# Earlier loads and shorter stage boundaries around the latent attention of a hybrid decoder, with six extra multiplications by TensorE in a wait

## The reference, cut to what matters

```
h = rmsnorm(x)
u = h @ w_in                       # columns: SSD | RWKV-7 | latent attention (MLA)
o_ssd, o_rwkv, o_mla = three mixers on u
gates = sigmoid(h @ w_gate + b_gate)
x = x + (gates0*(o_ssd@w_o_ssd) + gates1*(o_rwkv@w_o_rwkv) + gates2*(o_mla@w_o_mla)) @ w_out
x = x + ConvFFN(rmsnorm(x))
```

```
k = rmsnorm([c @ w_kb, rope_key]);  sc = q . k * scale           # per head, all 16 pages and the new tokens
pr = softmax(sc);  acc = pr @ c;  o_mla = acc @ w_vb
```

## Time and profile before

| what | value |
|---|---|
| median of 3 runs | 2997.09 us (2993.64 to 3005.37) |
| the profiled execution's own time | 2993.64 us |
| its span | 2991.5 us |
| TensorE busy | 2687.4 us, 90% |
| VectorE busy | 1881.6 us, 63% |
| ScalarE busy | 1351.0 us, 45% |
| GpSimd busy | 843.0 us, 28% |
| mean granted TensorE clock | 0.946 of full speed |

### The profile page before, as it was taken

The page is one execution under the profiler, slowest core; times in us unless marked ns, Lnnn a source line. Parts: engine busy times, 40 slices in busy tenths (PEclk is TensorE's granted clock), DMA queues, the critical chain, the costliest instruction groups (busy, mean ns, idle before and its releaser), DMA issues. The chain is left out here.

```text
span 2991.5 us, 62010 instructions
## 1 busy us (share of the span) xinstructions
PE 2687.4 (90%) x24068; PEld 2459.3 (82%) x24068; DVE 1881.6 (63%) x3141; ACT 1351.0 (45%) x2290; POOL 843.0 (28%) x696
## 2 busy tenths in 40 slices
PE   7986879999989889899988878799999798898998
PEld 6876449999988589899877863599999795898998
DVE  4854456777766655489358454477777575554993
ACT  4733354545444244354366334355555352434542
POOL 0030007999930400000000300099999104000000
PEclk9999879999998999999989989799999898999999
DMA  5324329877545376455453243497867244764644
GB/s 134 106 63 127 112 50 163 144 123 122 83 77 159 93 199 169 113 156 144 115 128 87 75 131 103 88 152 126 139 95 116 55 144 119 189 164 105 164 137 124
DMA packets 838310, 365.86 MB, mean 122 GB/s; under 512 B 406125, under 2 KB 825494, under 8 KB 837448
## 3 DMA queue, kind: packets, MB, share of 16 engines
q1 hardware_dynamic: 835794, 360.77, 52.7%
q10 hardware_dynamic: 2232, 1.26, 0.2%
HBM read 342.63 MB, written 61.23 MB: 135 GB/s over the span
## 5 line engine op out<-in xcount | busy, mean ns | idle before, releaser
L1196 PE MATMUL key_banks<-w_kb_head,latent_T_head 128*128 128x352 f32 x1536 | 520.5, 339 | 32.1 <-DVE latent_T_rest L1343 27.6
L1196 PE MATMUL key_banks<-w_kb_rest,latent_T_head 128*128 128x352 f32 x1536 | 496.9, 323 | 0.0
L1196 PE MATMUL key_banks<-w_kb_head,latent_T_rest 128*128 128x352 f32 x1536 | 496.2, 323 | 0.0
L293 DVE TENSOR_TENSOR w_rests<-w_ring,w_heads 128x2048 fp32r<-128x2048 f32 (+1 forms) x152 | 326.4, 2150 | 166.7 <-ACT w_heads L287 166.4
L1196 PEld LDWEIGHTS key_banks<-w_kb_head,latent_T_head 128*128 128x128 f32 x1536 | 291.4, 190 | 46.1 <-issue 29.7
L1357 DVE TENSOR_REDUCE w_kb<-key_sq 128x8 f32<-128x1024 f32 x256 | 311.0, 1215 | 12.3 <-ACT key_sq L1269 7.7
L978 POOL TENSOR_TENSOR rwkv_state_tmp<-rwkv_state,vec 128x1024 f32<-128x1024 f32 x64 | 154.5, 2414 | 509.0 <-DMA rwkv_state<-in_state_rwkv_dram 504.1
L287 ACT CAST w_heads<-w_ring 128x2048 fp32r<-128x2048 f32 (+1 forms) x152 | 272.3, 1794 | 54.6 <-ACT conv_last_rows L1899 19.7
L1196 PEld LDWEIGHTS key_banks<-w_kb_rest,latent_T_head 128*128 128x128 f32 x1536 | 291.8, 190 | 0.0
L1196 PEld LDWEIGHTS key_banks<-w_kb_head,latent_T_rest 128*128 128x128 f32 x1536 | 290.4, 189 | 0.0
L1256 ACT CAST latent_T_head<-turn_bank 128x256 fp32r<-128x256 f32 x256 | 95.5, 373 | 412.2 <-PE key_banks L1200 384.4
(11 more groups left out here) (587 smaller groups left out, 6998.7 us busy)
## 6 DMA issues: line engine op xcount, KB each, us to landing
w_ring<-in_ffn_w_up_dram SPq DMA_DIRECT2D x88, 512.0 KB, 5.0
page_latents<-in_cache_kv_latent_dram SPq DMA_DIRECT2D x256, 128.0 KB, 2.4
latent_blocks<-page_latents SPq DMA_DIRECT2D x256, 128.0 KB, 3.7
latents<-page_latents SPq DMA_DIRECT2D x64, 512.0 KB, 8.8
w_ring<-in_w_in_dram SPq DMA_DIRECT2D x52, 512.0 KB, 3.7
w_ring<-in_w_gate_dram SPq DMA_DIRECT2D x48, 512.0 KB, 3.9
w_ring<-in_w_in_dram SPq DMA_DIRECT2D x20, 1024.0 KB, 6.4
w_ring<-in_ffn_w_down_dram SPq DMA_DIRECT2D x32, 384.0 KB, 3.2
```

What stands on the lines that cost most here:

```text
L293: ops.tensor_tensor(rests[:, slot, 0:tiles * P], ring[:, slot, 0:tiles * P], heads[:, slot, 0:tiles * P].bitcast(F32), ALU.subtract).then_ ...
L1196: last = nc.tensor.matmul(kbank[:, 3 * x + n, 0:KB], c[:, x, r * P:(r + 1) * P], w[:, r, cols], start=r == 0 and m == 0, stop=r == 1 and m ...
```

## The change

The diff has eight parts.

1. `rwkv_tiles`: the prompt's state goes to a buffer of its own, and SP does not wait for its store; the wait stands at the end of `mla_project`. SP loads the first quarter of the first MLA weights in `rwkv_tiles`, behind the page copies.
2. `mla_project` does not wait for its four stores; ScalarE waits for them in `mla_qkv`, ahead of its first write to their source.
3. `mla_prompt` copies eight pages in place of ten and loads the sample's RWKV states; the other two pages are copied in `cache_attention`.
4. `mla_absorb` makes the head and rest of `w_kb` and of the first two sequences' queries, and SP loads there the first two blocks, half of the first rope blocks and the sample's rows. The sixteen small instructions on the new scores become two.
5. `cache_attention` begins with the pages; four small constants are made behind the third transpose.
6. `acc @ w_vb` and its copy move to the start of `ssd_project`, into bank 6.
7. `merge`: the weights of its first unit come in four transfers. The first half of the unit (g = 0) is rounded and split in two pieces, TensorE waits for these alone, and for the second half behind it.
8. In the last sequence's tail TensorE makes six products of the identity with 512 columns of constants into a bank of the keys, which nobody reads, before it waits for the maxima.

```diff
-GATHER = {..., "prompt": range(79, 89), "cache": range(89, NB * PAGES)}
+GATHER = {..., "prompt": range(79, 87), "cache": range(87, NB * PAGES)}
@@ rwkv_tiles, sync
                 copied = gather_pages(sp, k, GATHER["tiles"], gathered)
+                sp.dma_start(k.first_w[:, :, :], k.ldram("w_in")[0:2 * P, OFF_MLA:OFF_MLA + 256]...).then_inc(k.first_in, 16)
                 sp.wait_ge(kept["st"], 2)
-                sp.dma_start(..., state_rows).then_inc(st_out, 16)
-                sp.wait_ge(st_out, 16)
+                sp.dma_start(..., state_rows[:, :, :]).then_inc(k.state_stored, 16)
@@ mla_project, sync
-                for q in range(4):
+                for q in range(1, 4):
...
-                sp.wait_ge(stored, 64)
+                sp.wait_ge(k.state_stored, 16)
@@ mla_qkv, scalar
+                act.wait_ge(k.latents_stored, 64)
                 turned_out(0)
@@ mla_prompt, sync
+                for b in range(NB):
+                    sp.dma_start(k.state[b:P:NB, :, :]..., k.ldram("state_rwkv")[b:b + 1]...).then_inc(k.rows_back, 16)
                 copied = gather_pages(sp, k, GATHER["prompt"], gathered)
@@ mla_absorb, sync
+                load_blocks(sp, k, 0)
+                load_rope_blocks(sp, k, 0, 0)
+                sp.dma_start(k.vec[:, :, :, :]..., k.vec_rows...).then_inc(k.rows_back, 16)
+                load_blocks(sp, k, 1)
@@ mla_absorb, scalar
+                nc.scalar.copy(k.wh[:, :, 32:32 + KW], k.w_kb[:, :, :]).then_inc(w_heads, 1)
                 act.wait_ge(new_made, 1)
...
+                act.wait_ge(qa_kept, 2)
+                for b, cols in enumerate(FIRST_QUERIES):
+                    nc.scalar.copy(k.wh[:, :, cols], k.qa[:, :, b, :]).then_inc(k.q_headed, 1)
@@ mla_absorb, vector
+                dve.wait_ge(w_heads, 1)
+                nc.vector.tensor_tensor(k.wl[:, :, 32:32 + KW], k.w_kb[:, :, :], k.wh[...].bitcast(F32), ALU.subtract)
                 dve.wait_ge(made, 1)
...
-                for b in range(NB): ... tensor_tensor(out, banks[...b...], bc(ss, NS), ALU.mult)
-                for b in range(NB): ... tensor_tensor(out, out, mask[...b...], ALU.add)
+                c(nc.vector.tensor_tensor(out, banks[0:NSAM, 7, 0:256]..., bc(ss[:, :], NS)..., ALU.mult))
+                c(nc.vector.tensor_tensor(out, out, mask..., ALU.add))
@@ cache_attention, tensor, finish
                     if at == TURN_TOP:
+                        if is_last(b):
+                            pe.wait_ge(taken, NB * PAGES - 1)
+                            for _ in range(6):
+                                nc.tensor.matmul(kbank[:, 0, :], k.col("ident"), k.const[:, 0:BANK], start=True, stop=True, skip_group_check=True)
                         pe.wait_ge(topped, b + 1)
...
                 seqs(pe, body, finish)
-                pe.wait_ge(divided, NB)
-                for h in range(HEADS): for r in range(2): matmul(mbank..., k.w_vb..., acc...)
@@ ssd_project, tensor and vector
+                for h in range(HEADS): for r in range(2): matmul(banks[:, 6, ...], k.w_vb..., k.qa...)
+                last.then_inc(vmade, 1)
                 for u in range(NU):
...
                 nc.vector.tensor_tensor(y, y, bc(stat2[:, :], 64), ALU.mult).then_inc(normed, 1)
+                dve.wait_ge(vmade, 1)
+                nc.vector.tensor_copy(k.o_mla[:, :, SEQ:T], banks[:, 6, 0:HEADS * NSAM]...).then_inc(v_kept, 1)
                 rest_unit(nc.vector, dve, ring, heads, rests, rounded, split, 0, 1)
@@ merge, tensor, scalar and vector
+                            if u == 0 and g == 0 and t % 4 == 0:
+                                pe.wait_ge(piece_split, t // 4 + 1)
...
-                heads_of(0)
+                for q in range(2):
+                    act.wait_ge(piece_in[q], 16)
+                    nc.scalar.copy(piece(heads, q), piece(ring, q)).then_inc(piece_rounded, 1)
+                act.wait_ge(loaded[0], 32)
+                nc.scalar.copy(heads[:, 0, 2 * HALF:4 * HALF], ring[:, 0, 2 * HALF:4 * HALF]).then_inc(rounded, 1)
...
-                rests_of(0)
+                for q in range(2):
+                    dve.wait_ge(piece_rounded, q + 1)
+                    nc.vector.tensor_tensor(piece(rests, q), piece(ring, q), piece(heads, q).bitcast(F32), ALU.subtract).then_inc(piece_split, 1)
+                dve.wait_ge(rounded, 1)
+                nc.vector.tensor_tensor(rests[:, 0, 2 * HALF:4 * HALF], ...).then_inc(split, 1)
```

More of the change, by code:

```diff
@@ L1022, in cache_attention @@
     GROUPS = len(VALUES)
-    BLK = 3
     AHEAD = 3
@@ L1229, in finish @@
                                          start=True, stop=True, skip_group_check=True).then_inc(folded, 1)
-                pe.wait_ge(w_split, 1)
-                pe.wait_ge(ready, 4)
                 seqs(pe, body, finish)
-                pe.wait_ge(divided, NB)
-                for h in range(HEADS):
-                    for r in range(2):
-                        last = nc.tensor.matmul(mbank[:, h * 32:(h + 1) * 32], k.w_vb[:, r, h * P:(h + 1) * P],
-                                                acc[:, r, :, h * NS:(h + 1) * NS], start=r == 0, stop=r == 1, skip_group_check=True)
-                last.then_inc(vmade, 1)
             @block.scalar
             def _(act):
-                nc.scalar.copy(wh[:, :, 32:32 + KW], k.w_kb[:, :, :]).then_inc(w_heads, 1)
                 def query(b, slot):
                     nc.scalar.copy(wh[:, :, query_cols(slot)], k.qa[:, :, ds(b, 1), :].rearrange("p r o c -> p r (o c)")).then_inc(q_headed, 1)
-                query(0, 0)
-                query(1, 1)
-                act.wait_ge(w_split, 1)
                 def head(b, j):
@@ L1464, in _ @@
             def _(pe):
+                for h in range(HEADS):
+                    for r in range(2):
+                        last = nc.tensor.matmul(banks[:, 6, h * NSAM:(h + 1) * NSAM], k.w_vb[:, r, h * P:(h + 1) * P],
+                                                k.qa[:, r, :, h * NS:(h + 1) * NS], start=r == 0, stop=r == 1, skip_group_check=True)
+                last.then_inc(vmade, 1)
                 for u in range(NU):
@@ L1625, in merge, with piece @@
         squared, summed, inverse, y_ready = (st.sem(n) for n in ("squared", "squares_summed", "inverse_root", "ssd_normed"))
+        HALF = DT * P // 2
+        piece_in = [st.sem(f"first_piece_loaded{q}") for q in range(2)]
+        piece_rounded, piece_split = st.sem("first_pieces_rounded"), st.sem("first_pieces_split")
+        def piece(buf, q):
+            return buf[:, 0, q * HALF:(q + 1) * HALF]
         def gate_tile(u):
```

220 lines of the change are left out of this document (118 added, 102 removed).

## The result

The changed kernel takes 2953.38 us, the median of four runs (2951.6 to 2956.12). The kernel before, on the same chip, takes 2997.36 (four runs, 2993.64 to 3005.37). The ratio is 0.9851, 95% interval 0.9829 to 0.9872: 44 us faster, 38 to 51 by the interval. Predicted were 2946 in a range of 2932 to 2966, and faster with 0.94. The profiled execution took 2951.6 (span 2949.8, mean granted clock 0.957).

What follows compares the result with a forecast made beforehand. TensorE, busy for 90% of the span, was taken as the bound, so only idle time at boundaries could be gained. Terms of 24.0 and 24.1 us a layer, together 48.1, from 2993.64 gave 2945.5, predicted as 2946, range 2932 to 2966.

Steps and rivals of the forecast that it cites:

- A: Start of the MLA stage: without waiting for the state store and with first weights loaded, 3.0 us gained a layer.
- B: End of `mla_project`: the next stage starts earlier without the wait for four stores, 1.1 us a layer (0.8 to 1.2).
- C: `mla_prompt`: SP's eight loads for two page copies cost 0, or up to 2 us if they hold it up.
- D: `mla_absorb` to the pages' start: moved heads, rests and loads let pages start earlier, 9.2 us in layer 1, 8.6 in layer 2.
- D': Second block in the page loop: TensorE's stall goes as block and states are there, 1.9 and 2.6 us by layer.
- E: `acc @ w_vb` at the start of `ssd_project`: values run in the weights' shadow, first SSD product 4.8 us earlier a layer.
- F: First unit of `merge`: first half starts at once, second half earlier, 4.0 us gained a layer (3.1 to 4.6).
- G: Six products in the last sequence's tail: 0 gained, weighted sums still at half clock; ends 3.2 gain and 3.8 loss.
- rival 2: Stage boundaries: transfers issued earlier land no earlier, and `mla_prompt` ends 2 late; 11.7 us less gain, 2957; chance 0.16.
- rival 1: Last sequence's tail: the six products keep the clock up for weighted sums and values, 3.2 us a layer, 2939; chance 0.13.
- Rival 3: Page loop: its rhythm breaks as VectorE's work becomes longer; at 0.25 us a page the kernel takes 3010; chance 0.03.
- Rival 4: Pages' start and values: something the timeline does not show holds the boundary, 21 us gain left, 2973; chance 0.05.

Runs made afterwards that it cites:

- second profile: The kernel before and the changed kernel, each unchanged, profiled once more: one run of 3008.3 us before, median 2954.31 us of five for the changed kernel.
- version with ten products: Changed kernel with eight identity products in place of six before the maxima and two more behind their spread: 2946.32 us, ratio 0.9824 to the kernel before.
- version with fill: Changed kernel with ten tail products, plus four 512-column products between the value products at the start of `ssd_project`: 2960.64 us, ratio 0.9864 to the kernel before.

## Why the prediction was right

In us for each layer:

| term | predicted | measured | from |
|---|---|---|---|
| A state store, first MLA weights | 3.0 | 2.7 to 3.3 | all waits for MLA weights, 20.5 to 15.0 (layer 1: 9.74 to 6.12, less 0.75 more ahead of a later piece); 3.3 with the waits back |
| B four stores | 1.1 | 0.9 | 4.46 to 3.60 |
| C `mla_prompt` | 0 | 0, or a loss of 2.4 | wait 1.10 to 3.50 in layer 2 of the first profile |
| D pages' start | 9.2, 8.6 | 6.9 to 9.3, mean 8.3 | `mla_absorb` to first key product: 26.95, 26.38 (second profile 26.48, 27.14) to 17.83, 19.47 (18.53, 17.84) |
| D' second block | 1.9, 2.6 | 0.9 to 3.7, mean 2.8 | stall gone; first to last key product 429.30, 431.81 (431.82, 431.77) to 428.36, 428.79 (428.08, 428.31) |
| E values | 4.8 | 5.1 | values moved back |
| F `merge` | 4.0 | 3.4 to 3.7 | whole unit; sums' start to second half 14.83 to 11.12 |
| G six products | 0 | loss of 0.7 to 1.2 in ten layers of 14, none or a gain of up to 1.2 in four | without them |

For two layers the middle values give 43 to 46, against the 48 predicted and the 44 of the medians. The spread of the single terms is mostly the clock's, so that they meet the 44 so closely is in part luck.

*What bounds.* The reading that only TensorE's idle time at boundaries could be given back held: its busy time did not fall. But the page loop did not quite keep its rhythm: it loses 1.1 to 1.6 a layer, a cost that no term of the sum has. It hides in D', where more came back than the stall: in three of the four layers of before the clock also fell once behind the stall, and in none of the changed kernel.

*The boundaries.* In the mean of the layers A, B, D and D' came out within 0.6 of the step's working. The chain from the new scores to the first key product was read rightly. Single layers differ more: D gives 6.9 where `mla_absorb` ran at the lower clock behind SP's late end. Two of the reasons are thinner than I put them: the queue at the second block was relieved twice over, and the loads alone held the start almost as long as both together, the heads for two thirds of it.

*The values.* The size is right, the working was partly luck. I took 5.23 for the values, from an execution in which a part ran at full clock; in all later profiles they run at half clock for most or all of their time. The first SSD product then stands right behind them, as predicted, but in layer 1 it comes 25.1 behind the last key product and not the 23.2 worked out, 1.8 later. That the old place would have cost as much more makes up for it.

*The six products.* The step named the right reason (a second idle stretch behind them) and put the clock's fall ahead of the weighted sums, where it was. What it missed is what the clock does next. Without them the clock has already fallen and recovers in part before the values; with them it falls later, and in ten layers of 14 all of the folds and values are slow. The Trainium skill's "TensorE: Matmul & The Clock Gate", section "What's actually happening", makes the throttled state the default that activity releases. The version with ten products bears that out as far as the weighted sums (1.00), and the values, with TensorE busy for 6.00 of 6 at 0.50, do not.

*`mla_prompt`.* Here I took 0 with up to 2 as the other end, and said I would be wrong on the mechanism if SP ended it. It did in one layer of the first profile. Why not always: behind its first instruction of the stage TensorE is done after 29.9 to 37.2 us, by the clock, and SP after 31.3 to 32.8; in the kernel before SP was done after 29.6 to 29.8, so eight loads for two page copies made its work 2 to 3 us longer. Only behind the fastest attention (29.9, in two of the 20 layers with this stage) is SP last by more than 0.2. The cost is 2.4 and a slower `mla_absorb`. The fast attention itself made the stage 4.8 shorter in that layer of the first profile; that is no effect of a term. Of rival 2 this part was right; `merge` (3.1) and MLA (2.3) fell short of what was measured, and the stall at the second block did not stay.

*Rivals.* Of rival 1 only the worth of a kept clock was right. Rival 3 was right that the rhythm of the pages can change, and wrong by far on the size: about 0.01 us a page (1 us in 80 pages) and not 0.25. TensorE is the engine that is slower in it, with no idle time, and not VectorE. The sign that I named for it, pages of more than 3.1 us, was badly chosen: 80 pages in 268.2 us are 3.35 a page in the kernel before, since the softmax and weighted sums stand between the pages; after it is 3.37. Rival 4 fell with every boundary starting earlier.

## What to carry to other kernels

At a stage boundary look at who enters it last, SP included, and count what starts only behind it: loads, roundings and small products can be moved across one at a time, but where two chains stand side by side most of the gain comes only when both are moved. In this kernel filling idle time to keep the clock up paid only where it reached up to the work that should run fast; half a fill moved the fall onto useful work in most layers. When a change of a few us a layer is measured, read it from the stage that it touches and in more than one profile, since untouched stages move by up to 6 us from one execution to the next. And compare the long loops too, however untouched they look: 1 us in 268 repeated in every profile here, and no wait shows it.

## What the runs showed of the hardware

- The granted clock can stay at half while TensorE's row shows it busy without a gap: 7.00 of 7 us twice behind the start of `ssd_project` in the version with fill, and 12.00 of 12 in `ssd_tiles` without the six products. In both cases it had fallen in an idle stretch just before. The layers with the second fall take 81 us for `ssd_tiles` in place of 74 to 75; it is there in some executions and not in others.
- Products of 128x512 between products of 128x32 did not bring the clock back for 14 us, while in the tail the clock, full before them, stayed at 1.00 over them.
- An issue of a transfer is not always cheap for SP. Of the four issues at 431.36, 128 KB each, three take 0.55 to 0.73 us and one 2.68, and two of the next blocks' issues take 4.72 (row below) and 4.92, where one page copy of 128 KB takes 0.50. What is queued on SP behind such an issue waits with it.

```profile
453.93 4.72 SPq L900 DMA_DIRECT2D latent_blocks<-page_latents  x1
```
